# The opening of a hybrid decoder block: x handled tile by tile, two weight chunks projected half by half

## The reference

```python
h = rmsnorm(x, norm_w)          # y = x * rsqrt(mean(x*x) + eps) * w
z = h @ w_in                    # 1024 x 11264 columns, 88 chunks of 128
hq, hf, hi, hg, aqkv, ag, gates = jnp.split(z, IN_SPLITS, axis=-1)
f = lb + (1.0 - lb) * jax.nn.sigmoid(hf)
o_a = hgrn2_chunked(silu(hq), 1.0 - f, jnp.log(f), hi)   # 8 heads
...                             # dilated attention, gates, three more products
return x + merged @ w_out       # and a final rmsnorm
```

## Time and profile before

| | us |
|---|---|
| median of three runs | 1700.18 (1700.11 to 1707.92) |
| span of the profiled execution | 1706.1 |
| PE busy in it | 1673.4 (98%) |
| DVE, ACT, POOL busy | 814.6 (48%), 680.1 (40%), 105.2 (6%) |
| PE's first instruction | 17.5 |

### The profile page before, as it was taken

One profiled execution on the slowest core, in us unless ns is written; L12 is line 12 of the kernel. 1 busy time (PEld: TensorE's weight loads), 2 busy tenths in 40 slices (PEclk: granted clock), 3 DMA queues, 4 the chain that ended last, 5 costly groups with the idle time before them and its releaser, 6 DMA issues. The chain is left out here.

```text
span 1706.1 us, 21991 instructions
## 1 busy us (share of the span) xinstructions
PE 1673.4 (98%) x8564; PEld 1351.5 (79%) x8564; DVE 814.6 (48%) x1238; ACT 680.1 (40%) x834; POOL 105.2 (6%) x58
## 2 busy tenths in 40 slices
PE   4999999999999999999999999999999999999998
PEld 4788888888888888887777777777777777778897
DVE  5855454545454544538323561356324652444433
ACT  5646464555555555543322242224222332411221
POOL 3930000000000000001000000000000000000000
PEclk9999999999999999999999999899999997799999
DMA  5111111112111111123211121102201121232521
GB/s 194 38 62 50 63 49 61 49 45 66 37 56 54 49 61 49 61 75 86 64 37 50 50 63 51 50 25 62 76 25 50 50 94 51 80 117 99 191 100 74
DMA packets 33892, 113.73 MB, mean 67 GB/s; under 512 B 5338, under 2 KB 5788, under 8 KB 33820
## 3 DMA queue, kind: packets, MB, share of 16 engines
q1 hardware_dynamic: 33828, 112.82, 20.6%
HBM read 81.77 MB, written 18.45 MB: 59 GB/s over the span
## 5 line engine op out<-in xcount | busy, mean ns | idle before, releaser
L626 PE MATMUL z_ps<-h_hi,w_hi 128*128 128x512 f32 x1392 | 564.6, 406 | 0.0
L628 PE MATMUL z_ps<-h_hi,w_lo 128*128 128x512 f32 x1392 | 552.0, 397 | 0.0
L627 PE MATMUL z_ps<-h_lo,w_hi 128*128 128x512 f32 x1392 | 551.8, 396 | 0.0
L626 PEld LDWEIGHTS z_ps<-h_hi,w_hi 128*128 128x128 f32 x1392 | 264.4, 190 | 62.1 <-issue 0.6
L628 PEld LDWEIGHTS z_ps<-h_hi,w_lo 128*128 128x128 f32 x1392 | 263.6, 189 | 62.5
L627 PEld LDWEIGHTS z_ps<-h_lo,w_hi 128*128 128x128 f32 x1392 | 264.5, 190 | 56.8
L1211 DVE TENSOR_TENSOR w_lo<-w_stage,w_hi 128x1024 fp32r<-128x1024 f32 x87 | 106.9, 1228 | 308.6 <-ACT w_hi L955 308.6
L963 ACT ACTIVATE zz<-z_ps 128x512 f32<-128x512 f32 x48 | 28.7, 598 | 232.9 <-PE z_ps L628 177.0
L963 ACT ACT_TABLE_LOAD x61 | 78.3, 1283 | 88.7 <-PE z_ps L628 87.9
L1116 ACT ACTIVATE pt<-pb 128x512 f32<-128x512 f32 (+1 forms) x80 | 43.5, 544 | 149.7 <-PE pb L773 120.9
L790 PE MATMUL pc<-pt,vb 128*128 128x128 f32 x560 | 94.1, 315 | 0.0
(11 more groups left out here) (246 smaller groups left out, 2367.1 us busy)
## 6 DMA issues: line engine op xcount, KB each, us to landing
w_stage<-w_in SPq DMA_DIRECT2D x88, 512.0 KB, 3.4
z_swap<-zz SPq DMA_DIRECT2D x96, 128.0 KB, 2.3
gate_d<-gate SPq DMA_DIRECT2D x16, 512.0 KB, 3.8
x_in<-x SPq DMA_DIRECT2D x8, 512.0 KB, 8.1
o_a_d<-o_a SPq DMA_DIRECT2D x8, 512.0 KB, 4.7
w_stage<-w_a SPq DMA_DIRECT2D x8, 512.0 KB, 3.3
cos_t<-gate_d SPq DMA_DIRECT2D x8, 512.0 KB, 3.2
sin_t<-gate_d SPq DMA_DIRECT2D x8, 512.0 KB, 4.3
```

What stands on the lines that cost most here:

```text
L626: nc.tensor.matmul(z_ps[hf][:], w_hi[s][:, k, :], h_hi[:, k, t], start=k == 0, stop=False)
L627: nc.tensor.matmul(z_ps[hf][:], w_hi[s][:, k, :], h_lo[:, k, t], start=False, stop=False)
L628: last = nc.tensor.matmul(z_ps[hf][:], w_lo[s][:, k, :], h_hi[:, k, t], start=False, stop=k == KT - 1)
```

## The change

- `norm_w` is loaded as one row repeated on all 128 partitions (`norm_row`, in the memory of `dd[0]`), 512 KB in place of 4 KB, as the third large load; x tile 1 is issued ahead of it.
- Each tile is handled by itself: ACT squares it and takes the root; DVE takes the reciprocal and multiplies the tile by it and by `norm_row` in one `scalar_tensor_tensor`; PE transposes its eight channel tiles into two banks (of `pa`, `pb`, `pc` in turn); ACT copies each bank to `h_hi`, DVE makes `h_lo`.
- PE transposes tiles 0 to 3, then projects chunks 0 and 1 on the first token half in four quarters of 12 matmuls with a tile's transposes behind each, then both chunks on the second half. Chunk c now uses `z_ps[c]` for both halves, so the second half waits for ACT to empty the bank.
- ACT empties the four banks behind the last copy, and only then splits chunk 2. The first head's slots 0 to 3 have no projection.

```diff
@@ SP
             load_x(0)
-            for s, src in ((ident, "c_ident"), (norm_w, "norm_w")):
-                sp.dma_start(s[:], d[src]).then_inc(const_in, 16)
-            for t in range(1, 4):
+            load_x(1)
+            sp.dma_start(norm_row[:], d["norm_w"].to_broadcast([P, D_MODEL])).then_inc(const_in, 16)
+            sp.dma_start(ident[:], d["c_ident"]).then_inc(const_in, 16)
+            for t in range(2, 4):
                 load_x(t)
@@ POOL
-            pool.wait_ge(xt_made, 2 * KT)
+            pool.wait_ge(xt_made, 2 * NB)
@@ PE
-            def x_transpose(u):
...
+            def x_transpose(t):
+
+                pe.wait_ge(xn_done, t + 1)
+                for q in range(2):
+                    if t >= 3:
+                        pe.wait_ge(h_lo_done, 2 * (t - 3) + q + 1)
+                    for k in range(4):
+                        last = nc.tensor.transpose((pa, pb, pc)[t % 3][:, q, P * k:P * (k + 1)],
+                                                   x_in[:, t, P * (4 * q + k):P * (4 * q + k + 1)], ident[:])
+                    last.then_inc(xt_made, 1)
...
+            for t in range(4):
+                x_transpose(t)
+            pe.wait_ge(h_lo_done, NB)
+            for c in range(2):
+                pe.wait_ge(w_lo_done, c + 1)
+                first_project(c, 0, range(4))
+                x_transpose(4 + 2 * c)
+                first_project(c, 0, range(4, KT))
+                x_transpose(5 + 2 * c)
+            pe.wait_ge(h_lo_done, 2 * NB)
+            for c in range(2):
+                pe.wait_ge(z_taken[c], 1)
+                first_project(c, 1, range(KT))
...
-                        if not first(i) or slot >= 2:
+                        if not first(i) or slot >= 4:
@@ ACT
-            act.wait_ge(const_in, 32)
             def square(t):
...
+                act.wait_ge(ss_act, t + 1)
+                nc.scalar.activation(x_rms[:, t:t + 1], x_ss[:, t:t + 1], ACT.Sqrt, scale=1.0 / D_MODEL, bias=col[:, 2:3]).then_inc(rms_done, 1)
...
             square(0)
+            square(1)
+            for t in range(NB):
+                take_x(t)
+                if t + 2 < NB:
+                    square(t + 2)
+                if t in (1, 3):
+                    split_hi(t // 2, t // 2)
+            for hf in range(2):
+                for c, (dst, func) in enumerate(((ff, ACT.Sigmoid), (qq, ACT.Silu))):
+                    act.wait_ge(z_made[c], hf + 1)
+                    nc.scalar.activation(dst[:, HALF * hf:HALF * (hf + 1)], z_ps[c][:], func).then_inc(z_taken[c], 1)
...
+                    if first(i) and c == 0:
+                        continue
-                        take(i * HG_CHUNKS + c, hf, *evacs[c])
+                        if not first(i) or c > 1:
+                            take(i * HG_CHUNKS + c, hf, *evacs[c])
@@ DVE
+            def normalise(t):
+
+                dve.wait_ge(rms_done, t + 1)
+                nc.vector.reciprocal(x_rs[:, t:t + 1], x_rms[:, t:t + 1]).then_inc(rs_done, 1)
+                dve.wait_ge(rs_done, t + 1)
+                nc.vector.scalar_tensor_tensor(x_in[:, t, :], x_in[:, t, :], x_rs[:, t:t + 1], norm_row[:], ALU.mult, ALU.mult).then_inc(xn_done, 1)
+
+            normalise(0)
+            normalise(1)
+            for t in range(NB):
+                for q in range(2):
+                    dve.wait_ge(h_hi_done, 2 * t + q + 1)
+                    ks, ts = slice(4 * q, 4 * q + 4), slice(P * t, P * (t + 1))
+                    nc.vector.tensor_tensor(h_lo[:, ks, ts], (pa, pb, pc)[t % 3][:, q, :].rearrange("p (k t) -> p k t", t=P),
+                                            h_hi[:, ks, ts].bitcast(f32), ALU.subtract).then_inc(h_lo_done, 1)
+                if t + 2 < NB:
+                    normalise(t + 2)
```

More of the change, by code:

```diff
@@ L124, in build @@
         col = place("col", [P, 4])
-        norm_w = place("norm_w", [P, KT])
+        spare = place("spare", [P, KT])
         w_stage = [place(f"w_stage{s}", [P, KT, P]) for s in range(2)]
@@ L185, in build @@
         x_sq = lf
+        norm_row = dd[0]
         level_in, mask_t_in, sel_in = gg, vv, vv
@@ L251, in build @@
         x_loaded = [sem(f"x_loaded{t}") for t in range(NB)]
-        ss_act, ss_dve, rms_done, rs_done, xn_done = (sem(n) for n in ("ss_act", "ss_dve", "rms_done", "rs_done", "xn_done"))
+        ss_act, rms_done, rs_done, xn_done = (sem(n) for n in ("ss_act", "rms_done", "rs_done", "xn_done"))
         xt_made, h_hi_done, h_lo_done = sem("xt_made"), sem("h_hi_done"), sem("h_lo_done")
@@ L591, in _ @@
         def _(pe):
-            def x_transpose(u):
[L594 to L600, removed]
-            pe.wait_ge(const_in, 32)
[L604 to L617, removed]
@@ new lines, in first_project @@
+            def first_project(c, hf, ks):
+                t = slice(HALF * hf, HALF * (hf + 1))
+                for k in ks:
+                    nc.tensor.matmul(z_ps[c][:], w_hi[c][:, k, :], h_hi[:, k, t], start=k == 0, stop=False)
+                    nc.tensor.matmul(z_ps[c][:], w_hi[c][:, k, :], h_lo[:, k, t], start=False, stop=False)
+                    last = nc.tensor.matmul(z_ps[c][:], w_lo[c][:, k, :], h_hi[:, k, t], start=False, stop=k == KT - 1)
+                if k == KT - 1:
+                    last.then_inc(z_made[c], 1)
@@ L929, in square, with take_x @@
                 if t:
-                    act.wait_ge(ss_act, ACT_SQUARES.index(t))
+                    act.wait_ge(ss_act, t)
                 nc.scalar.activation(x_sq[:], x_in[:, t, :], ACT.Square, accum_out=x_ss[:, t:t + 1]).then_inc(ss_act, 1)
[L933 to L948, removed]
+                act.wait_ge(ss_act, t + 1)
+                nc.scalar.activation(x_rms[:, t:t + 1], x_ss[:, t:t + 1], ACT.Sqrt, scale=1.0 / D_MODEL, bias=col[:, 2:3]).then_inc(rms_done, 1)
+            def take_x(t):
+                for q in range(2):
+                    act.wait_ge(xt_made, 2 * t + q + 1)
+                    nc.scalar.activation(h_hi[:, 4 * q:4 * q + 4, P * t:P * (t + 1)],
+                                         (pa, pb, pc)[t % 3][:, q, :].rearrange("p (k t) -> p k t", t=P), ACT.Copy).then_inc(h_hi_done, 1)
             def split_hi(n, s):
-                if not isinstance(n, int) or n >= 2:
+                if isinstance(n, int) and n == 2:
+                    act.wait_ge(z_made[0], 2)
+                elif not isinstance(n, int) or n > 2:
                     act.wait_ge(z_made[1], n - 1)
@@ L1021, in hgrn @@
                     c, hf = slot // 2, slot % 2
-                    if cur and hf == 0 and not (first(i) and c == 0):
+                    if first(i) and c == 0:
+                        continue
+                    if cur and hf == 0:
                         split_hi(i * HG_CHUNKS + c + 1, (c + 1) % 2)
@@ L1291, in hgrn_cur @@
                 if slot == 2:
-                    for s in range(2):
-                        dve.wait_ge(z_taken[s], i * HG_CHUNKS + 1)
+                    if first(i):
+                        dve.wait_ge(z_taken[0], 2)
+                    else:
+                        for s in range(2):
+                            dve.wait_ge(z_taken[s], i * HG_CHUNKS + 1)
                     head = bass.ds(i, 1)
```

12 lines of the change are left out of this document (1 added, 11 removed).

## The result

| | before | changed |
|---|---|---|
| median, us | 1707.3 (1700.11 to 1719.08, 14 runs) | 1721.73 (1706.26 to 1728.03, 14 runs) |
| span of the profiled execution | 1706.1 | 1718.3 |
| ratio | | 1.0071, 95% interval 1.0046 to 1.0096 |

The changed kernel is slower: by 12.1 us from the ratio (0.0071 x 1707.3), with 7.9 to 16.4 as its interval, and by 14.4 between the medians. Forecast were 10.5.

The account below looks back on a forecast made before the run. PE, busy 98%, was taken as the bound, with a DVE string nearly as long beside it. The steps moved the level product from 78.4 to 88.9, 10.5 us later; on the median 1700.2 that gave 1710.7, range 1702 to 1718.

Parts of the forecast that it names:

- step 6: Second token half: 48 matmuls in 11.2 us to 53.7; DVE's split_lo of chunk 2 at 55.5; PE stands 3 us.
- step 5: New PE wait before the second half, for ACT to empty z_ps[0]: 2.7 us, ending at 42.5.
- first rival: "The DVE string shortens": POOL's rope steps get ahead, PE's 5.5 and 4.1 us waits vanish, total 1699.7; chance 0.22.
- Step 1 and 2: Loads and tile 0: norm_row there at 9.9, DVE normalises until 11.3, PE begins 6 us earlier.
- Step 3: Tiles 1 to 3 through ACT and DVE: 8.7 us plus 0.5 and 0.8 for POOL; h_lo of tile 3 at 24.4.
- Step 4: Four quarters of 12 matmuls with transposes: 14.0 us, plus 1.4 (half of 2.9) for the low clock; end 39.8.
- Step 7: DVE string bounds from split_lo, 32.0 us to the level product; PE waits 5.5 and 4.1; 87.5, with clock 88.9.
- last clock term: PE's clock falling once more in a long wait before the level product: 0 to 2.9 us, taken 1.4.
- Still slower, with the clock in full,: Rival: clock low in full at both places (+3.0) and POOL bound met (+1.4), total 1715; chance 0.14.
- the POOL bound: In tiles 1 to 3, DVE's multiplication waiting for all of POOL's w_lo: up to 2.2 us, 0.8 taken.
- Tiles do not flow: Rival: ACT and DVE wait for each other on every tile, 3.9 us per tile, total 1714; chance 0.06.
- The drain of the table load: Rival: a drain of about 1.38 us on the table switch before the second half, total 1712.1; chance 0.03.

Follow-up runs that it names:

- rope steps late: Changed kernel, but POOL starts its 20 rope steps only after DVE's first two picks; median 1710.38 us, ratio to before 1.0012.
- the four traces above: Changed kernel, and it with rope steps late, with chunk 2 split early, with 21 small transposes added; medians 1721.73, 1710.38, 1715.2, 1720.19 us.
- take early: Changed kernel, but ACT empties the bank of chunk 0's first half behind tile 5; median 1722.56 us, ratio to before 1.0094.
- both: Changed kernel with chunk 2 split early and the first bank emptied behind tile 5; median 1718.5 us, ratio to before 1.0045.
- all three: Changed kernel with chunk 2 split early, first bank emptied behind tile 5 and POOL's rope steps late; median 1706.65 us, ratio to before 0.9995.
- all three with PE warmed: The kernel with all three mends plus 21 useless small transposes between PE's early transposes; median 1703.82 us, ratio to before 0.9964.
- those with PE warmed: 21 useless small transposes added to the changed kernel (1720.19 us, ratio 1.0058) and to the one with all three mends (1703.82 us, 0.9964).
- early split: Changed kernel, but ACT splits chunk 2 before emptying chunk 1's last bank; median 1715.2 us, ratio to before 1.0050.

## Why the prediction was off

The time missed by 11.0 us, and two terms of the sum failed. One is the base: 7.1 of the 11.0. The other is in step 6, whose 48 matmuls were given 11.2 us at the high clock, with no clock term behind the new wait of step 5; they took 14.2. The mechanism held in its main line: the projections in the new order no longer cover DVE's string, and the loss of 10.5 us forecast was 12.1 by the ratio (7.9 to 16.4). What the sum did not see is why the string is so dear: it took the 32.0 us as given, and 12 of them are POOL's (20.7 with the rope steps late), a share that only the first rival had priced, at 10.6.

- **The base.** The sum was put on 1700.2, the median of three runs, though the profiled execution spanned 1706.1, and 1716.6 stood beside it. The later median is 1707.3. On it, 10.5 give 1717.8, still 3.9 below the measured time. The three runs were 1700.1, 1700.2 and 1707.9: a scatter of 8 us that the range should have carried.
- **Step 1 and 2** held: first transpose at 10.38 (forecast 11.3).
- **Step 3**: 24.4 forecast, 22.99 measured. 0.9 of the 1.4 us was the earlier start, and POOL took 0.3 us from one multiplication, not 0.8.
- **Step 4**: end of tile 7's transposes forecast 39.8, measured 40.7, 17.7 us behind the start of the first quarter in place of 15.4. That quarter cost 2.5 us more for the low clock, where half of 2.9 was taken for the whole step. That 39.8 came so near is luck: the errors of steps 3 and 4 nearly cancel.
- **Step 5**: the wait of 2.7 us was measured as 2.74 and ended at 43.45 for 42.5.
- **Step 6**: this is the step that failed. Behind the wait the clock fell, and 48 matmuls took 14.2 us in place of 11.2 (43.45 to 57.6). `split_lo` began at 59.29 and not at 55.5: 3.0 of these 3.8 us are the clock. That it fell is not a rule for this wait, as the four traces above show; a term from 0 to 3 us was due. PE's wait of 3 us was 3.1.
- **Step 7**: the string was 32.9 us for 32.0. PE's two waits were 0.9 and 6.2 in place of 5.5 and 4.1: PE, at the low clock behind chunk 2's wait, was itself 2.9 late for `k_out`, and `k_out` was done 16.4 us behind the start of `split_lo` and not 18.0. The sum at the product is not touched by that. The clock behind it cost 2.6 (half of 92.19 to 97.4) in place of 1.4; with it the product's 13.8 become the mark's 16.1, near enough.

At the product the forecast was 87.5 before its last clock term, the measured 92.19: 3.8 of the difference stood already at `split_lo`, 0.9 came from the string.

**The rivals.** *The DVE string shortens* did not occur: `k_out` came 1.6 us sooner behind `split_lo`, but PE still waited for it, and the string was not shorter. Its premise held only in small part: the steps from POOL's second to its seventh took 17.3 us with DVE idle for most of them (44.07 to 61.34) and 19.7 in before (45.36 to 65.06), and the last step ended at 97.7, where 87 was named as a sign. What it had right is the size on DVE's side: 11 of 33 us, by the late rope steps. *Still slower, with the clock in full,* is the nearest to what was measured, 14.9 us above its base, but only half for its reasons: the clock was low at both places (2.5 and 2.6 us of 2.9), the POOL bound was not met (0.3 for 2.2), and the 3.0 us in step 6 stood in no rival. *Tiles do not flow*: they did, at about 3 us per tile (`h_lo` of tile 0 done at 13.7, of tile 3 at 22.9). *The drain of the table load* did not appear: ACT's activation followed the load at once, as in the kernel before.

**The two rules.** What the Trainium skill (ScalarE: Activation LUTs, What ACT_TABLE_LOAD costs) says of a drain is not borne out: at 41.41 the load begins, right behind the last copy, and at 42.71 the activation. What the Trainium skill (SBUF — State Buffer, Who interferes with whom) says of DVE instructions with two SBUF inputs beside POOL agrees with the largest effect here: with POOL's rope steps away, DVE's busy time in the string fell from 31.65 to 20.37 us. But the prediction left out a condition of its other half: the Trainium skill (SBUF — State Buffer, Who interferes with whom) frees an instruction with one SBUF input only outside DVE's 2-port modes. By the rows, instructions with one SBUF input have a share: `tensor_scalar` for `kk`, in the changed kernel and with the rope late,

```profile
61.84 2.75 DVE L1300 TENSOR_SCALAR kk<-ff 128x1024 f32<-128x1024 f32 x1
```

```profile
59.22 0.69 DVE L1301 TENSOR_SCALAR kk<-ff 128x1024 f32<-128x1024 f32 x1
```

and the copy of `k_one` took 1.17 and 0.43 us. Which instruction waited for which was not tried, nor in which mode these ran.

## What to carry to other kernels

An engine's wait that is removed at the front is worth only what the other engines' strings let through: before merging two stages, look at which string the second stage was covering, and compare its length with what is left above it. A slowdown between two engines that costs nothing under cover becomes the bound when the cover goes. Here moving POOL's side work was worth as much (12.3 us at the product) as giving the new order up (11.7). Where the clock can fall behind a wait, every new wait on the path needs a clock term of its own. And a forecast of a time needs the scatter of the base in its range, not only the doubts about the change.

## What the runs showed of the hardware

- The granted clock at one and the same wait of 2.74 us fell in two traces of four, and cost up to 3 us; behind the wait of 1.57 us in the same place it fell in none of four (take early, both, all three, all three with PE warmed). Around waits of 3.6 to 5.6 us for `k_out` it fell in four of four, and PE then took 4.6 to 6.0 us longer over the same work. In two traces (those with PE warmed) the clock fell inside a run of matmuls, about 0.4 and 1.3 us after PE had stood for 2.3 us.
- The clock column of a trace can read 1.00 where the matmuls have the step of the low level: 12 matmuls in 5.3 us in the changed kernel from 22.99 on.
- POOL's `tensor_scalar` on 128x1024 takes very different times beside an idle DVE: 2.79 us at 47.80 (one multiplication), 1.05 at 42.93, with DVE on tiny operands only (multiplication and addition). I did not look for the reason.
- DVE's string up to its first pick took 32.1 to 33.1 us in all seven kernels of the changed order that have POOL's rope steps beside it, whenever it began (49.51 to 59.29), and 20.7 without them; with the early split and the early bank as well it took 24.5, of which 4.3 is one wait for ACT.
